# A two-block language model on one core: attention pairs in three units, a folded final norm and wide token weights

## The reference

```
def rms_norm(x, g): return x * rsqrt(mean(x * x) + 1e-6) * g
x = rms_norm(h, final_norm)                      # end of the first block
for i in range(2):                               # the second block
    z = rms_norm(x, norm_g[i]) @ w_in[i]
    qa, ka, va, ga, fa, qb, kb, vb, gb = split(z)
    c = cumsum(log_sigmoid(fa + b_f[i]))         # 8 forget gates, one a head
    oa = softmax(norm(qa) @ norm(ka).T / 8 + c_q - c_k, causal) @ va * silu(ga)
    ob = dilated(rope(norm(qb)), rope(norm(kb)), vb) * silu(gb)
    x = x + concat(oa, ob) @ w_out[i]
    x = x + (p[i] @ w_ple[i]) * sigmoid(rms_norm(x, ple_norm_g[i]) @ w_ple_gate[i])
```

## Time and profile before

| quantity | value |
|---|---|
| median of three runs | 3533.19 us (3532.7 to 3535.07) |
| the profiled execution, its own time | 3537.04 us |
| its span, first to last instruction | 3535.2 us |
| PE, PEld, DVE, ACT busy | 96%, 78%, 48%, 39% of the span |
| TensorE's mean granted clock | 0.984 of full speed |
| chain that ended last, by engine | PE 89%, DVE 5%, ACT 4%, issue 1% |

### The profile page before, as it was taken

One profiled execution on the slowest core, in us unless ns is written; L12 is line 12 of the kernel. 1 busy time (PEld: TensorE's weight loads), 2 busy tenths in 40 slices (PEclk: granted clock), 3 DMA queues, 4 the chain that ended last, 5 costly groups with the idle time before them and its releaser, 6 DMA issues.

```text
span 3535.2 us, 39297 instructions
## 1 busy us (share of the span) xinstructions
PE 3406.6 (96%) x16632; PEld 2754.0 (78%) x16632; DVE 1699.5 (48%) x2267; ACT 1374.4 (39%) x1828; POOL 52.6 (1%) x116
## 2 busy tenths in 40 slices
PE   8999999999999999999999999999999998999889
PEld 7888877887688888888877987788878865888657
DVE  5443367644544334443367544444335455644554
ACT  5222257333432223222267233432225445454443
POOL 0000000100000000000001000000000000000000
PEclk9999999999999999999999999999999989999999
DMA  4222211022122222222211032122221210222102
GB/s 162 96 90 93 92 60 60 13 96 95 48 96 96 87 104 96 95 89 94 92 60 48 13 108 84 60 96 96 90 104 60 85 47 9 93 84 84 36 19 84
DMA packets 46895, 275.04 MB, mean 78 GB/s; under 512 B 5248, under 2 KB 8576, under 8 KB 21504
## 3 DMA queue, kind: packets, MB, share of 16 engines
q1 hardware_dynamic: 46720, 272.52, 21.5%
HBM read 270.41 MB, written 2.10 MB: 77 GB/s over the span
## 4 chain that ended last, share of the span: by engine, by line
PE 89%; DVE 5%; ACT 4%; issue 1%; DMA 0%; SPq 0%; DVEq 0%; ACTq 0%
PE banks L293 73%; PE banks L1450 1%; PE banks L2236 1%; PE banks L1464 1%; PE banks L2248 1%; PE banks L1462 1%; PE banks L1292 1%; PE banks L1279 1%; ACT slab_hi L275 1%; PE banks L2561 1%; PE banks L2059 1%; PE banks L925 1%; DVE row_max L2316 1%; DVE slab_lo L282 1%; PE banks L1306 1%
## 5 line engine op out<-in xcount | busy, mean ns | idle before, releaser
L293 PE MATMUL banks<-x_hi,slab_hi 128*128 128x512 f32 x2688 | 1065.7, 396 | 16.8 <-DVE x_lo L374 16.8
L293 PE MATMUL banks<-x_lo,slab_hi 128*128 128x512 f32 x2688 | 1049.9, 391 | 0.0
L293 PE MATMUL banks<-x_hi,slab_lo 128*128 128x512 f32 x2688 | 1049.9, 391 | 0.0
L275 ACT ACTIVATE slab_hi<-slab_raw 128x2048 fp32r<-128x2048 f32 (+2 forms) x276 | 483.9, 1753 | 1087.2 <-PE banks L293 1076.7
L282 DVE TENSOR_TENSOR slab_lo<-slab_raw,slab_hi 128x2048 fp32r<-128x2048 f32 (+2 forms) x276 | 577.3, 2092 | 444.5 <-ACT slab_hi L275 444.4
L293 PEld LDWEIGHTS banks<-x_hi,slab_hi 128*128 128x128 f32 x2688 | 506.1, 188 | 134.1 <-issue 28.4
L293 PEld LDWEIGHTS banks<-x_lo,slab_hi 128*128 128x128 f32 x2688 | 506.2, 188 | 112.5 <-issue 7.2
L293 PEld LDWEIGHTS banks<-x_hi,slab_lo 128*128 128x128 f32 x2688 | 505.7, 188 | 107.6
L293 PE MATMUL banks<-hidden_hi,slab_hi 128*128 128x512 f32 x704 | 279.1, 396 | 0.0
L293 PE MATMUL banks<-hidden_lo,slab_hi 128*128 128x512 f32 x704 | 279.1, 396 | 0.0
L293 PE MATMUL banks<-hidden_hi,slab_lo 128*128 128x512 f32 x704 | 279.1, 396 | 0.0
(11 more groups left out here) (335 smaller groups left out, 4299.2 us busy)
## 6 DMA issues: line engine op xcount, KB each, us to landing
slab_raw<-slabs SPq DMA_DIRECT2D x196, 1024.0 KB, 4.8
slab_raw<-slabs SPq DMA_DIRECT2D x64, 704.0 KB, 4.0
slab_raw<-slabs SPq DMA_DIRECT2D x16, 640.0 KB, 3.8
h<-xT SPq DMA_DIRECT2D x8, 256.0 KB, 5.7
memory<-memT SPq DMA_DIRECT2D x2, 1024.0 KB, 5.5
out<-h SPq DMA_DIRECT2D x8, 256.0 KB, 4.3
constants<-con SPq DMA_DIRECT2D x1, 1408.5 KB, 10.1
memory_in<-memT SPq DMA_DIRECT2D x1, 1024.0 KB, 14.6
```

The lines of the kernel that those rows point to most:

```text
L275: self.nc.scalar.activation(self.wh[:, g % self.HIGHS, 0:w], self.raw[:, g % self.RAWS, 0:w], ACT.Copy).then_inc(self.hi_ready, 1)
L293: mm = self.nc.tensor.matmul(out, left[a], right[c], start=start and n == 0, stop=stop and n == 2)
```

## The change

Attention: the 4 query blocks of a pair become 3 units, blocks 0 and 1 side by side in one bank (384 columns), block 2 (384) and block 3 (512). Reductions, exponentials, scalings and copies are still one per block (`exp` and `scale` loop over `blocks(u)` too, with one increment a head). The reduction negates its result itself. The odd head's weights are turned into bank 7, which `out` uses too, and the even head's into bank 6. The bias covers a whole unit: for forgetting heads the key sums have the first 128 keys once more in front, the causal table is 384 wide with zeros in its middle; the dilated tables are 768 wide. `take` moves ahead of the copies of a pair's first unit, and that unit's bias ahead of its odd turn.

Final norm: `FinalNorm` goes. `FoldedX` makes the next x from the unscaled h with the product of both gains (`FoldGains` multiplies them once), and sums two kinds of squares, of h and of h times the final gain. `FoldedNorm` makes both roots of them at slab 0 of the next projection, and h is scaled at slabs 8 to 15 as a side. Token products: hi and lo of the 8 columns lie side by side in one tile of 128 columns, x_hi and x_lo are multiplied by it (16 products), and the turning, now a matmul with 0/1 columns, adds the halves. All 128 rows are evacuated. The constants have 8 more columns, the bias tables four more steps.

```diff
+class FoldedX(NextX):
...
+    def scalar(self, act, c):
+        super().scalar(act, c)
+        k = self.k
+        if c >= 3:
+            act.wait_ge(*self.added.at(c - 2))
+        k.nc.scalar.activation(self.sum2[:] if c == 0 else self.sq2[:, c % 2, :], k.h[:, c, :], ACT.Square,
+                               scale=k.fin[:, c:c + 1]).then_inc(self.squared.sem, 1)
+    def vector(self, dve, c):
+        super().vector(dve, c)
+        if c >= 1:
+            dve.wait_ge(*self.squared.at(c + 1))
+            if c >= 2:
+                dve.wait_ge(*self.added.at(c - 1))
+            self.k.nc.vector.tensor_tensor(self.sum2[:], self.sum2[:], self.sq2[:, c % 2, :], ALU.add) \
+                .then_inc(self.added.sem, 1)
...
+    def norm_tensor(self, pe):
+        k, nc = self.k, self.k.nc
+        pe.wait_ge(k.sums, self.x.summed)
+        pe.wait_ge(*self.x.added.at(KC - 1))
+        for n, total in enumerate((k.sumsq, self.x.sum2)):
+            nc.tensor.matmul(k.ps[:, 7 - 2 * n, :], k.ones[:], total[:], start=True, stop=True)
+            for tb in range(TB):
+                mm = nc.tensor.matmul(k.ps[:, 6, TB * n + tb:TB * n + tb + 1], total[:, tb * P:(tb + 1) * P],
+                                      k.ones[:, 0:1], start=True, stop=True, skip_group_check=True)
+        mm.then_inc(k.total, 1)
+    def norm_scalar(self, act):
+        k, nc = self.k, self.k.nc
+        act.wait_ge(k.total, self.total0 + 1)
+        nc.scalar.activation(self.logs, k.ps[:, 7, :], ACT.Ln, scale=1.0 / D, bias=EPS).then_inc(self.scaled.sem, 1)
+        nc.scalar.activation(self.col_logs[:], k.ps[:, 6, 0:TB], ACT.Ln, scale=1.0 / D, bias=EPS) \
+          .then_inc(self.scaled.sem, 1)
+        act.wait_ge(*self.scaled.at(2))
+        nc.scalar.activation(k.rstd[:], self.logs, ACT.Exp, scale=-1.0).then_inc(self.scaled.sem, 1)
+        nc.scalar.activation(k.rcol[:], self.col_logs[:], ACT.Exp, scale=-1.0).then_inc(self.scaled.sem, 1)
+        nc.scalar.activation(self.first, self.logs, ACT.Exp, scale=-0.5).then_inc(self.scaled.sem, 1)
+        for n, a in enumerate((k.rstd, k.rcol)):
+            act.wait_ge(*self.made.at(n + 1))
+            nc.scalar.activation(a[:], a[:], ACT.Ln, scale=1.0 / D, bias=EPS).then_inc(self.scaled.sem, 1)
+        act.wait_ge(*self.made.at(4))
+        nc.scalar.activation(k.rstd[:], k.rstd[:], ACT.Exp, scale=-0.5)
+        nc.scalar.activation(k.rcol[:], k.rcol[:], ACT.Exp, scale=-0.5).then_inc(k.rstd_ready, 1)
+    def norm_vector(self, dve):
+        k, nc = self.k, self.k.nc
+        dve.wait_ge(*self.scaled.at(4))
+        nc.vector.tensor_tensor(k.rstd[:], k.rstd[:], k.ps[:, 5, :], ALU.mult).then_inc(self.made.sem, 1)
+        nc.vector.tensor_tensor(k.rcol[:], k.rcol[:], k.ps[:, 6, TB:2 * TB], ALU.mult).then_inc(self.made.sem, 1)
+        for n, (a, logs) in enumerate(((k.rstd, self.logs), (k.rcol, self.col_logs[:]))):
+            dve.wait_ge(*self.scaled.at(n + 6))
+            nc.vector.tensor_tensor(a[:], a[:], logs, ALU.add).then_inc(self.made.sem, 1)
+        dve.wait_ge(k.rstd_ready, self.ready)
+    def vector(self, dve, s):
+        k, c = self.k, s - self.FIRST
+        if c == 0:
+            dve.wait_ge(*self.scaled.at(5))
+        if 0 <= c < KC:
+            k.nc.vector.scalar_tensor_tensor(out=k.h[:, c, :], in0=k.h[:, c, :], scalar=k.fin[:, c:c + 1],
+                                             in1=self.first, op0=ALU.mult, op1=ALU.mult)
...
-                for n, (v, x) in enumerate(((self.hi, xh), (self.hi, xl), (self.lo, xh))):
-                    mm = nc.tensor.matmul(k.ps[:, 6, :], v[:, kk, :], x[:, kk, :],
-                                          start=n == 0 and kk == 0, stop=n == 2 and kk == KC - 1)
+                for n, x in enumerate(self.x):
+                    mm = nc.tensor.matmul(k.ps[:, 6, :], self.both[:, kk, :], x[:, kk, :],
+                                          start=n == 0 and kk == 0, stop=n == 1 and kk == KC - 1)
...
-                mm = nc.tensor.transpose(self.turned[:, tb, :], self.rows[:, tb * P:(tb + 1) * P],
-                                         k.c("ident")[0:8, 0:8])
+                mm = nc.tensor.matmul(self.turned[:, tb, :], self.rows[:, tb * P:(tb + 1) * P], k.c("sum_groups"),
+                                      start=True, stop=True, skip_group_check=True)
...
+    UNITS = 3
+    BLOCKS = ((0, 1), (2,), (3,))
+    WIDTH = (384, 384, 512)
...
+    def blocks(self, u):
+        at = 0
+        for tb in self.BLOCKS[u % self.UNITS]:
+            yield tb, slice(at, at + (tb + 1) * P)
+            at += (tb + 1) * P
...
         def score(u):
-            if u >= 3:
+            if u >= self.UNITS:
                 pe.wait_ge(*self.exp_done.at(2 * (u - 2)))
-            for c in range(2):
-                self.scores(self.bank(u, c), *divmod(u, TB), c)
+            for n, (tb, at) in enumerate(self.blocks(u)):
+                for c in range(2):
+                    self.scores(self.bank(u, c)[:, at], u // self.UNITS, tb, c, n == 0)
         def add_bias(u):
             for c in range(2):
-                mm = self.bias(self.bank(u, c), *divmod(u, TB), c)
+                mm = self.bias(self.bank(u, c), u // self.UNITS, u % self.UNITS, c)
             mm.then_inc(self.z_ready.sem, 1)
         def turn(u, c):
-            for b in range(u % TB + 1):
-                mm = nc.tensor.transpose(ps[:, self.TURNED, b * P:(b + 1) * P],
-                                         self.weights(u, c)[:, b * P:(b + 1) * P], k.c("ident"))
+            pe.wait_ge(*self.p_ready.at(2 * u + 1 + c))
+            if u >= 1:
+                pe.wait_ge(*(self.pt_a, self.pt_b)[c].at(u))
+            if c and u % self.UNITS == 0 and u >= 1:
+                pe.wait_ge(*self.y_ready.at(u // self.UNITS))
+            for b in range(self.WIDTH[u % self.UNITS] // P):
+                block = slice(b * P, (b + 1) * P)
+                mm = nc.tensor.transpose(ps[:, 6 + c, block], self.weights(u, c)[:, block], k.c("ident"))
             mm.then_inc((self.turned_a, self.turned_b)[c].sem, 1)
         def out(p):
-            pe.wait_ge(*self.pt_a.at(TB * (p + 1)))
-            pe.wait_ge(*self.pt_b.at(TB * (p + 1)))
-            if p >= 1:
-                pe.wait_ge(*self.y_ready.at(p))
+            pe.wait_ge(*self.pt_a.at(self.UNITS * (p + 1)))
...
+        pe.wait_ge(k.bank_free, self.banks_ready)
         for u in range(3):
             score(u)
             add_bias(u)
         for u in range(units):
-            if u % TB == 0 and u >= TB:
-                out(u // TB - 1)
-            pe.wait_ge(*self.p_ready.at(2 * u + 2))
-            if u >= 1:
-                pe.wait_ge(*self.pt_b.at(u))
+            first = u % self.UNITS == 0 and u >= 1
+            if first:
+                out(u // self.UNITS - 1)
             turn(u, 0)
             if u + 3 < units:
                 score(u + 3)
-            pe.wait_ge(*self.pt_a.at(u + 1))
+                if first:
+                    add_bias(u + 3)
             turn(u, 1)
-            if u + 3 < units:
+            if u + 3 < units and not first:
                 add_bias(u + 3)
         out(pairs - 1)
...
         def top(u):
+            n = 2 * (u % self.UNITS)
             dve.wait_ge(*self.z_ready.at(u + 1))
             if u >= 3:
                 dve.wait_ge(*self.exp_done.at(2 * (u - 2)))
-            both = ps[:, 2 * (u % 3):2 * (u % 3) + 2, 0:self.cols(u)]
-            nc.vector.tensor_reduce(self.two(self.mx, u), both, AX.X, ALU.max).then_inc(self.max_ready.sem, 1)
-            dve.wait_ge(*self.max_ready.at(u + 1))
-            nc.vector.tensor_scalar(self.two(self.nm, u), self.two(self.mx, u), -1.0, None, ALU.mult).then_inc(self.neg_ready.sem, 1)
+            for tb, at in self.blocks(u):
+                ins = nc.vector.tensor_reduce(self.nm[:, 2 * tb:2 * tb + 2], ps[:, n:n + 2, at], AX.X, ALU.max,
+                                              negate=True)
+            ins.then_inc(self.neg_ready.sem, 1)
...
         def keep(u, c):
-            p, tb = divmod(u, TB)
+            p, n = divmod(u, self.UNITS)
             dve.wait_ge(*(self.turned_a, self.turned_b)[c].at(u + 1))
             if p >= 1:
                 dve.wait_ge(*self.o_ready.at(p))
-            col = c * self.HEAD + tb * P
-            to = self.pt[:, col:col + (tb + 1) * self.STEP].rearrange("p (b t) -> p b t", t=self.STEP)[:, :, 0:P]
-            of = ps[:, self.TURNED, 0:self.cols(u)].rearrange("p (b t) -> p b t", t=P)
-            nc.vector.tensor_copy(to, of).then_inc((self.pt_a, self.pt_b)[c].sem, 1)
+            for tb, at in self.blocks(u):
+                col = c * self.HEAD + tb * P
+                to = self.pt[:, col:col + (tb + 1) * self.STEP].rearrange("p (b t) -> p b t", t=self.STEP)[:, :, 0:P]
+                of = ps[:, 6 + c, at].rearrange("p (b t) -> p b t", t=P)
+                ins = nc.vector.tensor_copy(to, of)
+            ins.then_inc((self.pt_a, self.pt_b)[c].sem, 1)
...
```

(35 more changed lines are left out.)

255 lines of the change are left out of this document (133 added, 122 removed).

## The result

The changed kernel takes 3430.84 us (median of 4 runs, 3429.2 to 3435.6) beside 3534.13 us of the kernel before on the same chip (4 runs, 3532.7 to 3537.2). The ratio is 0.9709, with a 95% interval of 0.9692 to 0.9726. I had forecast 3473 us and a range of 3458 to 3501. The sign was right, the size was not. The profiled executions are 3537.0 us before and 3435.6 after, with spans of 3535.2 and 3433.9: 101.3 us less, where my sum said 60.5.

A forecast was written before the change was run, and what follows sets the result against it. PE, busy 96% of the span, bounds the kernel, with attention's pitch set by a ring of waits. Savings of 33.6 + 5.9 + 13.5 + 7.5 = 60.5 us from the 3533.2 median give 3473 us, range 3458 to 3501.

The forecast's parts named there:

- The attention ring: Attention steady pairs: a bank for each head and three units cut the pitch from 14.4 to 12.0 us, saving 33.6 us.
- eight hand-overs at 0.05: Attention pair: a term of some eight hand-overs between engines at 0.05 us each, bringing 11.5 to 12.0 us a pair.
- 14 pitches: Both attention stages: 14 distances between `out`, each shortened from 14.4 to 12.0 us, 33.6 us in all.
- The last `out` and its slow clock: End of each attention stage: the last `out`, 4.25 and 4.54 us, was left unchanged in the forecast.
- The ramps: Start of each attention stage to its first `out`: 17.5 us against 21.3 and 19.6, saving 5.9 us.
- The final norm: Last feed-forward product to the end of the second norm's sums: 27.66 us becomes 14.2, saving 13.5 us.
- the tokens: Token products on PE: four times 8 products of 0.233 us go, saving 7.5 us.
- The chain of roots: Folded norm: low part of slab 2 ends 11.5 us after the sums, PE asks at 14.7, so no cost.
- The queues' order: Rival, attention: waits in queue order hold the ring, pitch 13.4, saving 39 us, 3494 us; chance 0.16.
- The clock: Rival, attention: clock swings, half of PE's work at 1.2 GHz, 13.9 us a pair, 3501 us; chance 0.10.
- The rule weighed there: Attention on PE: small idle times between matmul groups cycling through PSUM banks let the clock swing; led to the 3501 us rival.
- The packed case: Rival, attention: work packs to the fullest engine, pitch 10.5, saving 85 us in all, 3448 us; chance 0.08.

The follow-up runs named there:

- the last kernel: Changed kernel with VectorE's copy of the odd head moved behind the reciprocal and the maximum at a pair's first unit; 3427.19 us, ratio 0.9686.
- the run with the region at 0: Changed kernel with 128 bytes more ahead of the shared region; 3452.6 us, ratio 0.9756.
- the kernel with one bank: Changed kernel, three units kept, with both heads turned through bank 6 and the waits of before; 3454.36 us, ratio 0.9758.

## Why the prediction was wrong, point by point

**The attention ring: right in kind, too long by 0.95 us.** The order of steps in the trace is the one I followed. From `out` to DVE's view of the odd head I had 5.2 and the trace has 4.97 (2862.42 to 2867.39); to ScalarE's scale 0.75 against 0.72; to DVE's reciprocal 3.13 against 2.98; from there to `out` 2.4 against 2.38. Together these are 11.05 against 11.48. The rest is the "eight hand-overs at 0.05", rounded up to 0.5. The trace's steps run from start to start, so they hold every hand-over, and each is shorter than my term for it: the terms, lengths of rows mostly, already came to more than the whole pair. Twelve pitches by 0.95 are 11.4 us. The step that failed is this sum, the same in kind and 0.95 us a pair too long, and the bank is the smaller part of what it saves.

**The last pair: the wrong count.** I multiplied 14 pitches. In the last pair no unit of a next pair stands in the ring, and it takes 7.49 in both stages. In the kernel before, the last pitch was 13.69 and 14.05, since its copies through one bank bound it too, and I carried that over. Two by 4.5 are 9.0 us.

**"The last `out` and its slow clock I leave as they are."** They went from 4.18 and 4.47 (to the next product's start) to 2.30 twice, 4.0 us. I argued that the clock would hold in the steady pairs, and didn't ask what it followed at the end. The ramps gave 4.8 instead of 5.9. In all the attention gave 62.8 us for 39.5 forecast: 11.4 + 9.0 + 4.0 - 1.1.

**The final norm and the tokens: right.** 13.4 us for 13.5, and 7.8 for 7.5 (24 * 0.233 before, 16 * 0.227 after; I had used the old distance for what goes, and nothing for the faster rest). The chain of roots is as drawn: the low part of slab 2 ends at 2650.12, 11.5 us after the sums at 2638.65, and PE asks for the token products at 2649.49 and comes to slab 2 only at 2654.43.

**The step that was not there.** I costed instructions, waits and queues, and let the tiles move for nothing: 96 bytes ahead of the shared region had no term. They are worth some 24 us, nearly a quarter of the result. The trace of before held the sign of it: products on x start 0.227 apart and those on hidden 0.234, on tiles of the same shape. I used the first distance for slab 0 and never asked why the two differ.

**Sum:** 23.3 of attention and 24.6 of placement, +0.3 of tokens, -0.1 of the norm, and 7.3 lost in other stages, most of it by the clock in the second mixer, are the 40.8 us that separate 60.5 from 101.3. The range ended 15 us under the forecast, so either of the first two alone would have passed it.

**The rivals.** The queues' order did not hold the ring: no pitch is above 11.06. The clock does not swing in steady pairs: 1.00 in the window of six, so half-speed stretches like the 0.75 of the earlier trace rows are gone. The rule weighed there (the Trainium skill, TensorE: Matmul & The Clock Gate, section "A second HAM failure mode: psum-queue depth-cycling") would have had the swing stay; this kernel's trace does not agree with it in steady state, where PE has records open for 92% of the time, and its longest wait of a pair is 0.89. The packed case was nearest, with 3448 us at 0.08. It had the pitch wrong in the other direction (10.5), and its bound of 10.5 was passed by the last kernel, with 10.4.

## What to carry to other kernels

When products of one shape have two different distances in a profile, find out why before costing anything: here 7 to 8 ns in 227 were worth some 24 us, by the offset modulo 256 bytes between the moving operand and the weights. When a change adds even 32 bytes ahead of a region, list which tiles move, and keep their offsets or cost the move. Look for moved tiles behind the profile's names too, which leave numbers out. In a ring, measure each step from start to start, which holds the hand-overs, and count the last turn apart, without the work of the next one.

## What the runs showed of the hardware that I had not expected

- Products of 128 rows by 512 columns (float32r, with weights reloaded for each) start 226.7 ns apart where the moving tile and the weight slab have the same start modulo 256 bytes, and 232 to 234 ns apart at six other pairs of starts (32, 64, 96, 160 and 0 against 128, and 128 against 0). Moving both together changes nothing.
- The mean is exact while single distances are not: in the run with the region at 0, the products alternate between 229 and 238 ns and give 233.3 over the stage, the same as at 64, 96 and 160, where single ones are 230 to 236.
- Time at the lower clock moves between executions of one kernel (mean clocks of 0.991 to 0.994 in four). In the kernel after, the clock was 1.00 over six pairs, with a wait of PE of up to 0.89 us before each `out`, and in the last pair too. In the kernel with one bank it fell to 0.50 in the last pair, behind waits of 0.93 and 0.81 us, and in one run it fell at the last `out` behind the same work as in the kernel after.
